# Twelve sigmoids of the second block as one Tanh pass each, and the meta tokens' state products on four row groups

## The reference

```python
proj = jnp.einsum('btd,dk->btk', u, w_in[l])
gates = jax.nn.sigmoid(proj[..., OFF_GATE:])
c = conf_a * jax.nn.sigmoid(conf_g)                 # the GLU
c = depthwise_conv(c, w_conf_dw[l], b_conf_dw[l])   # 31 taps
c = jax.nn.silu(layer_norm(c, conf_ln_g[l], conf_ln_b[l]))
branch_conf = jnp.einsum('btc,cd->btd', c, w_conf_out[l])
xbc = jax.nn.silu(depthwise_conv(xbc, w_ssm_conv[l], b_ssm_conv[l]))   # 7 taps
y = bidir_ssd(xs, dt_raw, ssm_dt_bias[l], ssm_a_log[l], Bs, Cs, ssm_d[l])
y = rms_norm_2(y * jax.nn.silu(z), w_ssm_norm[l])
branch_ssm = jnp.einsum('btc,cd->btd', y, w_ssm_out[l])
merged = gates[..., :D_MODEL] * branch_conf + gates[..., D_MODEL:] * branch_ssm
h = h + jnp.einsum('btd,de->bte', merged, w_out[l])
```

## Time and profile before

| | before |
|---|---|
| median of three runs | 1831.09 us |
| profiled execution, its own time | 1831.83 us |
| its span | 1830.1 us |
| TensorE busy with matmuls | 1724.3 us (94%) |
| VectorE busy | 708.0 us (39%) |
| ScalarE busy | 585.8 us (32%) |
| read from memory | 521.12 MB |

### The profile page before, as it was taken

How to read it: one execution, slowest core, us unless ns; L and a number is a source line. 1 busy time by engine, 2 the same in 40 slices (tenths; PEclk the granted TensorE clock), 3 DMA queues, 4 the chain that set the end, 5 groups by cost and what they waited for, 6 DMA issues and landing times.

```text
span 1830.1 us, 21256 instructions
## 1 busy us (share of the span) xinstructions
PE 1724.3 (94%) x8462; PEld 982.1 (54%) x8462; DVE 708.0 (39%) x1365; ACT 585.8 (32%) x1026; POOL 32.2 (2%) x58
## 2 busy tenths in 40 slices
PE   9999999999999999999999999998989889898997
PEld 8878788887878787777722322222222222222222
DVE  2584466603769999961221111122111211112112
ACT  1153132202365564650133332223222332223222
POOL 4000000000000000000000000000000000000000
PEclk9999999999999999999999999889999999999898
DMA  5340244442443434266879999999999999999996
GB/s 185 116 182 14 80 161 145 170 156 103 166 164 121 158 137 154 104 237 248 322 312 429 431 428 434 429 430 429 431 432 427 433 428 432 432 429 428 431 433 260
DMA packets 34511, 523.47 MB, mean 286 GB/s; under 512 B 3768, under 2 KB 3960, under 8 KB 6392
## 3 DMA queue, kind: packets, MB, share of 16 engines
q1 hardware_dynamic: 33200, 511.75, 68.2%
q10 hardware_dynamic: 1224, 10.50, 1.6%
HBM read 521.12 MB, written 1.12 MB: 285 GB/s over the span
## 4 chain that ended last, share of the span: by engine, by line
PE 60%; DMA 16%; DVE 14%; DVEq 3%; ACT 2%; another core or an unknown queue 2%; issue 1%; ACTq 0%; SPq 0%
PE psum L1181 18%; DMA arena<-in_experts 16%; PE psum L580 10%; PE psum L1153 9%; PE psum L926 5%; DVE arena L2065 4%; PE psum L899 4%; DVE arena L2053 2%; PE psum L1008 2%; PE psum L1165 2%; DVEq L2067 2%; PE psum L664 1%; PE psum L643 1%; PE psum L879 1%
## 5 line engine op out<-in xcount | busy, mean ns | idle before, releaser
L1181 PE MATMUL psum<-arena 128*34 128x512 f32 x2048 | 467.4, 609 | 43.6 <-DMA arena<-in_experts 38.7
L926 PE MATMUL psum<-arena 128*128 128x272 f32 x1344 | 313.9, 393 | 1.6 <-DVE arena L2273 1.6
L1181 PEld LDWEIGHTS psum<-arena 128*34 128x34 f32 x2048 | 120.9, 114 | 362.1 <-issue 313.8
L1692 DVE SCALAR_TENSOR_TENSOR arena<-psum,arena 34x512 f32<-34x512 f32 x64 | 44.2, 690 | 683.4 <-ACT arena L1253 683.4
L926 PEld LDWEIGHTS psum<-arena 128*128 128x128 f32 x1344 | 254.3, 190 | 56.5 <-DVE arena L2273 2.1
L1153 PE MATMUL psum<-arena 128*34 128x512 f32 x1024 | 249.1, 642 | 19.4 <-DMA arena<-in_experts 18.5
L580 PE MATMUL psum<-arena 128*128 128x256 f32 x992 | 215.4, 378 | 0.0
L580 PEld LDWEIGHTS psum<-arena 128*128 128x128 f32 x992 | 187.2, 189 | 27.6 <-issue 1.2
L1153 PEld LDWEIGHTS psum<-arena 128*34 128x34 f32 x1024 | 66.3, 119 | 189.9 <-issue 188.6
L1652 ACT ACTIVATE arena<-psum 34x512 f32<-34x512 f32 x64 | 37.9, 593 | 311.9 <-PE psum L1181 311.9
L2065 DVE SCALAR_TENSOR_TENSOR arena<-arena 128x272 f32<-128x272 f32 x240 | 112.1, 527 | 3.5
(11 more groups left out here) (427 smaller groups left out, 1439.3 us busy)
## 6 DMA issues: line engine op xcount, KB each, us to landing
arena<-in_experts SPq DMA_DIRECT2D x74, 4096.0 KB, 50.4
arena<-in_panels SPq DMA_DIRECT2D x91, 1024.0 KB, 4.8
arena<-in_experts SPq DMA_DIRECT2D x41, 2048.0 KB, 43.8
arena<-in_down_panels SPq DMA_DIRECT2D x8, 1408.0 KB, 6.1
arena<-scr ACTq DMA_DIRECT2D x4, 2176.0 KB, 9.1
arena<-in_experts SPq DMA_DIRECT2D x5, 1024.0 KB, 8.0
arena<-in_experts SPq DMA_DIRECT2D x2, 512.0 KB, 47.8
out<-arena SPq DMA_DIRECT2D x4, 256.0 KB, 2.1
```

The source lines that it names most:

```text
L926: ins = mm(pair[k][:, b, 0:T], slot8[k][:, c, b * P:(b + 1) * P], src[:, c, :], start=c == 0, stop=c == DC - 1)
L1181: ins = mm(psum[lo:lo + CAP, p % 2, :], xg[:, c, :], r_up[2 * p + x][:, c, :], start=c == 0, stop=c == DC - 1)
```

## The change

Two things change, both in the second block. First, every sigmoid but the one behind the layer norm becomes one Tanh of half the argument: sigmoid(x) = (1 + tanh(x/2)) / 2. ScalarE's Abs, Exp, Ln and second Exp become one Tanh (`half_tanh`), VectorE's subtraction goes, and its product becomes a product with the sum in it, (t + 1) * x, as one three-operand instruction. The halves go elsewhere: into the weights of both convolutions and one bias, which VectorE scales once at the start (two instructions of 248 and 192 elements), and into products that were there anyway (`gated`, `ssm_part`, the merge). Tanh is not in the table set that holds Ln, so ScalarE loads the set with Exp and Tanh behind the Ln of dt, and the old one ahead of the Ln of the norm behind the groups.

Second, `ssm_y` does the meta tokens' products ahead of the others, each with its 32 rows only, on row groups 0, 32, 64 and 96 of the array and into four banks.

```diff
...
@@ -430,7 +430,7 @@
                 if g == 1:
-                    sp.wait_ge(ev("gsig_ready"), after["gsig_ready"] + 2)
+                    sp.wait_ge(ev("gates_tanh"), after["gates_tanh"] + 2)
                     expert_panel(0, 10)
@@ -980,14 +980,16 @@
                 for b in range(4):
+                    rows = slice(32 * b, 32 * b + 32)
+                    mm(G[b][:, 0:T], xf[rows, 0, b * P:(b + 1) * P], m_f0[rows, :], start=True, stop=False, skip_group_check=True)
+                for b in range(4):
                     bank = G[b]
...
                             h = 2 * b + x
-                            mm(bank[64 * x:64 * x + 64, lo:hi], src[:, ck, h * 64:(h + 1) * 64], m[:, h, :],
-                               start=at == 0, stop=False, skip_group_check=True)
-                    ins = mm(bank[:, 0:T], xf[:, 0, b * P:(b + 1) * P], m_f0, start=False, stop=True, skip_group_check=True)
+                            ins = mm(bank[64 * x:64 * x + 64, lo:hi], src[:, ck, h * 64:(h + 1) * 64], m[:, h, :],
+                                     start=False, stop=at == 3, skip_group_check=True)
                     ins.then_inc(ev("y_done"), 1)
@@ -1465,9 +1467,9 @@
-            def arg_exp(tmp, name, count, done):
-                act.wait_ge(ev(name + "_arg"), count)
-                A(tmp, tmp, ACT.Exp).then_inc(ev(done), 1)
+            def half_tanh(tmp, x, done, scale=0.5):
+
+                A(tmp, x, ACT.Tanh, scale=scale).then_inc(ev(done), 1)
@@ -1510,8 +1512,8 @@
-            def z_ln(g):
-                sigmoid_ln(zt if g < 3 else zt_last, zT[:, 4 * g:4 * g + 4, :], "z")
+            def z_tanh(g):
+                half_tanh(zt if g < 3 else zt_last, zT[:, 4 * g:4 * g + 4, :], "z_tanh")
@@ -1528,6 +1530,7 @@
             A(dtw, dtw, ACT.Ln).then_inc(ev("dt_ln"), 1)
+            nc.scalar.preload_act_table_set("exp_and_others")
             act.wait_ge(ev("dtr_ready"), 1)
@@ -1543,9 +1546,8 @@
             act.wait_ge(ev("conv6"), after["conv6"] + 1)
-            sigmoid_ln(six, gq[0], "group")
+            half_tanh(six, gq[0], "six_tanh", 1.0)
             copy_mid(MID_OPEN[4:5])
-            arg_exp(six, "group", 1, "sig6")
             for g, bank in enumerate((G[0], G[1], G[3], G[2])):
@@ -1555,14 +1557,12 @@
                     act.drain()
-                    sigmoid_ln(glu_t, glu_gate(g), "glu")
+                    half_tanh(glu_t, glu_gate(g), "glu_tanh")
                 differences(g, 0)
...
                 own_decays(g)
-                if g < 2:
-                    arg_exp(glu_t, "glu", g + 1, "glu_exp")
                 copy_mid(MID_A[g][1:2])
@@ -1573,14 +1573,12 @@
                 act.wait_ge(ev("conv6"), after["conv6"] + g + 2)
-                sigmoid_ln(six, gq[(g + 1) % 2], "group")
+                half_tanh(six, gq[(g + 1) % 2], "six_tanh", 1.0)
                 copy_mid(MID_B[g][0:1])
...
                 act.drain()
-                z_ln(g)
-                arg_exp(six, "group", g + 2, "sig6")
+                z_tanh(g)
                 copy_mid(MID_B[g][1:2])
-                arg_exp(zt, "z", g + 1, "z_exp")
                 if g == 2:
@@ -1594,18 +1592,14 @@
             copy_mid(MID_A[3][1:2])
-            z_ln(3)
+            z_tanh(3)
             copy_mid(MID_A[3][2:3])
-            arg_exp(zt_last, "z", 4, "z_exp")
-            sigmoid_ln(gate_t, gts[:, 0:DC, :], "gates")
+            half_tanh(gts[:, 0:DC, :], gts[:, 0:DC, :], "gates_tanh")
             copy_mid(MID_A[3][3:4])
-            act.wait_ge(ev("gates_arg"), 1)
-            A(gts[:, 0:DC, :], gate_t, ACT.Exp).then_inc(ev("gsig_ready"), 1)
             squares(3)
             act.drain()
-            sigmoid_ln(gate_t, gts[:, DC:2 * DC, :], "gates")
-            act.wait_ge(ev("gates_arg"), 2)
-            A(gts[:, DC:2 * DC, :], gate_t, ACT.Exp).then_inc(ev("gsig_ready"), 1)
+            half_tanh(gts[:, DC:2 * DC, :], gts[:, DC:2 * DC, :], "gates_tanh")
+            nc.scalar.preload_act_table_set("natural_log_exp_and_others")
             act.wait_ge(ev("ssum_done"), after["ssum_done"] + 1)
@@ -1617,8 +1611,7 @@
             act.drain()
-            sigmoid_ln(conf_t, cc, "conf")
-            arg_exp(conf_t, "conf", 1, "csig_ready")
+            sigmoid(conf_t, cc, "conf").then_inc(ev("csig_ready"), 1)
             for i in range(4):
@@ -1718,6 +1711,8 @@
             TT(ident4, ident[:, 0:16], ident[:, 32:48], ADD)
+            for at, count in ((PAR["conf_w"], 248), (PAR["ssm_w"], 192)):
+                TS(par[:, at:at + count], par[:, at:at + count], 0.5, None, MUL)
             dve.drain()
@@ -2071,12 +2066,12 @@
             def glu_mul(x):
-                dve.wait_ge(ev("glu_exp"), after["glu_exp"] + x + 1)
-                TT(cpad[:, 4 * x:4 * x + 4, 15:15 + T], glu(x)[:, :, 0, :], glu_t, MUL).then_inc(ev("cpad_ready"), 1)
+                dve.wait_ge(ev("glu_tanh"), after["glu_tanh"] + x + 1)
+                STT(cpad[:, 4 * x:4 * x + 4, 15:15 + T], glu_t, 1.0, glu(x)[:, :, 0, :], ADD, MUL).then_inc(ev("cpad_ready"), 1)
             def silu(g):
-                dve.wait_ge(ev("sig6"), after["sig6"] + g + 1)
-                TT(gq[g % 2], gq[g % 2], six, MUL).then_inc(ev("g6_ready"), 1)
+                dve.wait_ge(ev("six_tanh"), after["six_tanh"] + g + 1)
+                STT(gq[g % 2], six, 1.0, gq[g % 2], ADD, MUL).then_inc(ev("g6_ready"), 1)
@@ -2172,13 +2167,13 @@
                 zg = zT[:, 4 * g:4 * g + 4, :]
-                dve.wait_ge(ev("z_exp"), after["z_exp"] + g + 1)
-                TT(zg, zg, tmp, MUL)
+                dve.wait_ge(ev("z_tanh"), after["z_tanh"] + g + 1)
+                STT(zg, tmp, 1.0, zg, ADD, MUL)
...
                 dve.drain()
-                TT(zg, zg, gq[g % 2][:, 0:4, :], MUL).then_inc(ev("yz_ready"), 1)
+                STT(zg, zg, 0.5, gq[g % 2][:, 0:4, :], MUL, MUL).then_inc(ev("yz_ready"), 1)
@@ -2187,15 +2182,12 @@
             meta_tables()
-            sigmoid_arg(six, gq[0], "group", 1)
             silu(0)
...
                 ssm_x(g, 2)
-                if g < 2:
-                    sigmoid_arg(glu_t, glu(g)[:, :, 1, :], "glu", g + 1)
                 ssm_e(g)
@@ -2208,10 +2200,8 @@
                 conf_taps(TAPS[g][2])
-                sigmoid_arg(six, gq[(g + 1) % 2], "group", g + 2)
+                silu(g + 1)
                 conf_taps(TAPS[g][3])
-                silu(g + 1)
-                sigmoid_arg(zt, zT[:, 4 * g:4 * g + 4, :], "z", g + 1)
                 conf_taps(TAPS[g][4])
@@ -2226,17 +2216,14 @@
             ssm_m(3)
-            sigmoid_arg(zt_last, zT[:, 12:16, :], "z", 4)
             conf_taps(TAPS[3][2])
             z_silu(3, zt_last)
-            sigmoid_arg(gate_t, gts[:, 0:DC, :], "gates", 1)
             ssm_out(3)
...
             fold(cc)
-            sigmoid_arg(gate_t, gts[:, DC:2 * DC, :], "gates", 2)
             centre()
@@ -2246,11 +2233,11 @@
                 part = gts[:, DC + 2 * i:DC + 2 * i + 2, :]
-                TT(part, part, pair[(base + i) % 2][:, :, 0:T], MUL).then_inc(copied[(base + i) % 2], 2)
-
-            dve.wait_ge(ev("gsig_ready"), after["gsig_ready"] + 2)
+                STT(part, part, 0.5, pair[(base + i) % 2][:, :, 0:T], MUL, MUL).then_inc(copied[(base + i) % 2], 2)
+
+            dve.wait_ge(ev("gates_tanh"), after["gates_tanh"] + 2)
             dve.wait_ge(ev("srs_ready"), after["srs_ready"] + 1)
-            TT(gts[:, DC:2 * DC, :], gts[:, DC:2 * DC, :], ssum.unsqueeze(1).to_broadcast([P, DC, T]), MUL)
+            STT(gts[:, DC:2 * DC, :], gts[:, DC:2 * DC, :], 1.0, ssum.unsqueeze(1).to_broadcast([P, DC, T]), ADD, MUL)
             dve.wait_ge(ev("sq_ready"), SQ["conf"] + 1)
@@ -2268,9 +2255,9 @@
                 part, of_conf = gts[:, DC + 2 * i:DC + 2 * i + 2, :], gts[:, 2 * i:2 * i + 2, :]
-                TT(of_conf, of_conf, pair[k][:, :, 0:T], MUL).then_inc(copied[k], 1)
-                dve.drain()
-                TT(bcf[:, 2 * i:2 * i + 2, :], of_conf, part, ADD).then_inc(ev("merged_ready"), 1)
+                STT(of_conf, of_conf, 1.0, pair[k][:, :, 0:T], ADD, MUL).then_inc(copied[k], 1)
+                dve.drain()
+                STT(bcf[:, 2 * i:2 * i + 2, :], of_conf, 0.5, part, MUL, ADD).then_inc(ev("merged_ready"), 1)
             base += 4
...
             v.memset(pos_t, 0.0)
```

More of the change, by code:

```diff
@@ L106 @@
              "g6_ready": ("g6_ready", 0), "gathered": ("dec_done", 2), "gathered_half": ("bias_ready", 1),
-             "glu_exp": ("rn_ln", 4), "gsig_ready": ("o_copied", 2), "h_ready": ("qk_ready", 1),
+             "glu_tanh": ("rn_ln", 4), "gates_tanh": ("o_copied", 2), "h_ready": ("qk_ready", 1),
              "hacc_turned": ("expG_done", 1), "htok_copied": ("probsT_copied", 6),
@@ L115 @@
              "rows_ready": ("st1_done", 1), "rst_ready": ("gsum_done", 1), "scattered": ("scattered", 0),
-             "sig6": ("ro_ready", 1), "sq_added": ("u_done", 2), "sqx_added": ("eps_ready", 1),
```

(3 more changed lines are left out.)

## The result

Beside each other on one chip, the changed kernel takes 1810.8 us (median of 4 runs, 1808.0 to 1814.9) and the kernel before 1833.65 us (4 runs): a ratio of 0.989, with a 95% interval of 0.9876 to 0.9903. On a second chip it was 1809.29 against 1831.43, ratio 0.9879 (0.9862 to 0.9895). The gain of 20 to 23 us is above the 16 that were forecast, and above the 14 to 19 that had 0.60. The profiled execution took 1808.04 us with a span of 1806.3, which is 23.8 us less than before.

A forecast was written before the change was run, and what follows sets the result against it. TensorE, plus its waits for VectorE, sets the pace of the groups; the weight stream bounds the experts. Waits of 9.5 and meta products of 6.4 make 15.9 us off 1831.83: 1815.9, median said as 1815, range 1808 to 1824.

The forecast's parts named there:

- the 14 to 19 that had 0.60: Main forecast for the whole kernel: gain 14 to 19 us, 1812 to 1817, chance 0.60, larger row-group overlap included.
- The waits: TensorE's five waits for VectorE: four inside the groups go, the variance sum's nearly, plus lower-clock time; 9.5 us.
- The leads: VectorE ahead of TensorE at `m_ready` in the groups: 4.7, 4.2 and 4.9 us, so the waits inside go.
- the waits move: Rival: late copies or decays hold the fourth group again; gain 10.3 or 6 us, 1821 to 1825; chance 0.14.
- The tangent: Sigmoids: Tanh priced like other ScalarE functions, VectorE's product with the sum like the plain one; nothing counted beyond the waits.
- Table loads: ScalarE's two added loads, behind dt's Ln and after the last gate: both hidden in idle time, 0 us.
- The meta tokens' products: In `ssm_y`, four products on row groups: 1.6 us saved per group, 6.4 in all, bounds 0.8 and 2.2.
- The sum: Whole kernel: waits 9.5 plus meta products 6.4 make 15.9 us, from 1831.83 to 1815.9; median said as 1815.
- No overlap: Rival on `ssm_y`: row groups bring no overlap; 12.7 us less, 1818.4, or 1821 with new-shape cost; chance 0.17.
- Nothing arrives: Rival: the experts' weight stream ends the kernel and its start does not move; 1831; chance 0.06.
- A slower clock behind `ssm_y`: Rival: quarter-row products lower TensorE's clock in the panels behind; 1845 at 30 us of such work; chance 0.03.

The follow-up runs named there:

- the tangent alone: The changed kernel with the `ssm_y` of before, so only the sigmoids' part: 1819.81 us against 1830.51, ratio 0.9946.
- the experiment with 24 more: The changed kernel with a table set change and back ahead of each of twelve Tanh, 24 extra loads: 1810.13 us in one run.
- the row groups alone: The kernel before with the new `ssm_y`, sigmoids as before: 1831.21 us against 1830.51, ratio 1.0005.

## Why the prediction was right, and where its sizes were off

**The waits: 9.5 forecast, 10.8 measured** (the tangent alone). The mechanism held to the row: all five gone, the first `ssm_y` at 534.95 (537 forecast). The size was low for two reasons: the idle brackets of the waits inside the groups understate them by 0.1 to 0.3 us each, and the two products behind the longest wait were at the lower clock too, 0.5 us, which I had not counted. Start to start, the pieces of before are longer than those of the changed kernel by 16.76 - 14.82 = 1.94 (bracket 1.87), 2.96 - 1.37 = 1.59 (1.32), 16.67 - 14.83 = 1.84 (1.78), and in the fourth group 4.81 - 1.37 = 3.44 (2.67, and the 0.5); the variance sum 8.63 - 7.55 = 1.08 (1.10). With the 0.89 of the two slow panels that is 10.8. The starts of before that are not in the earlier trace rows are:

```profile
521.97 14.89 PE L926 MATMUL psum<-arena 128*128 128x272 f32 x64
...
600.62 1.08 PE L977 MATMUL psum<-arena 128*128 128x272 f32 x4
...
603.58 14.89 PE L926 MATMUL psum<-arena 128*128 128x272 f32 x64
...
745.50 1.08 PE L977 MATMUL psum<-arena 128*128 128x272 f32 x4
```

**The leads.** VectorE's convolutions start at 530.37, 607.98 and 682.12 (532, 610 and 683 forecast), and the taps in the fourth group's place at 746.89 (747.8 forecast):

```profile
746.89 3.56 DVE L2060 SCALAR_TENSOR_TENSOR arena<-arena 128x272 f32<-128x272 f32 x8
```

The periods between them shrank by 3.9, 2.4 and 2.9 us (81.5, 76.6 and 67.7 before; 77.6, 74.1 and 64.8 now), where the lost subtractions alone were forecast to give 4.2, 3.0 and 3.0. So VectorE's side came close to the forecast. TensorE's did not: `m_ready` leads by 4.6, 2.9 and 4.6 us and in the fourth group by 1.0, where I had 4.7 for the first, 4.2 for the second and 4.9 for the fourth. TensorE asks in the fourth at 747.85 and not at 752.7. It was 2.0 us ahead of my forecast at the first `ssm_y` (1.8 of it the front's clock), and gained 2.9 more up to the fourth, through three `ssm_y` of 0.7 us less each and the waits, which were longer than their brackets. The rival "the waits move" was nearer than its 0.14 says: the product behind the last `x_ready` is done at 730.88 + 0.69 = 731.57, and TensorE asks for it ahead of the third of `ssm_cb`'s products, near 732.6 (731.65 and two products of 0.46). So both margins of the fourth group were 1.0 us, where the sum had given some 5 to the one at `m_ready`.

**The tangent.** One pass of 1632 elements takes 1.56 us like Exp and Ln, and VectorE's product with the sum takes what it did, as the earlier trace rows said.

```profile
546.21 1.56 ACT L1472 ACTIVATE arena<-arena 128x1632 f32<-128x1632 f32 x1 [10.52 <-DVEq L2050]
...
L2074 DVE SCALAR_TENSOR_TENSOR arena<-arena 128x1632 f32<-128x1632 f32 x4 | 7.4, 1858 | 0.2
```

**Table loads: 0 forecast, 0 measured.** The second one is at 761.20, and ScalarE then waits 7.55 us for TensorE's sum; the experiment with 24 more shows how wide the cover is.

```profile
761.20 1.28 ACT L1602 ACT_TABLE_LOAD   x1
770.04 0.49 ACT L1604 ACTIVATE arena<-psum,arena 128x272 f32<-128x272 f32 x1 [7.55 <-PE psum L596]
```

**The meta tokens' products: the term that was mis-sized.** I took 1.6 us per `ssm_y`, 6.4 in all, within bounds of 0.8 and 2.2. They gave 2.31 (8.55 - 6.24), 9.2 in all and outside the bounds. Two things were off. First, I held that the records' order allows only half of an overlap, since a product's second record runs on the same rows as its first. Eight records took 0.67 us, 84 ns each, against 1.93 us with full rows: 2.9 times as fast. The rule of the Trainium skill that I had weighed against it ("TensorE: Matmul & The Clock Gate", section "Measured speedup vs the span model", 3.07 times) was the better guide; the earlier trace rows, with 64-row products of 64 columns, was not the nearest row that I took it for. Second, I counted the cost of alternating at 0.2 us per full product and none in its neighbours, where the 64-column products got 0.4 us shorter too. (The other way, by 0.1: the last of the four full products took 0.57 and not 0.66.)

**The sum.** 10.8 and 4 x 2.31 = 9.2 make 20.0; 19.6 arrived between the two cuts. The 0.4 is in the panels behind each `ssm_y`, which now follow a 64-column product instead of a full one:

```profile
541.19 37.10 PE L926 MATMUL psum<-arena 128*128 128x272 f32 x160
```

These five take 36.93 us (541.19 to 578.12), where the earlier trace rows has 36.83 (547.28 to 584.11), and behind the other three it is 0.1 as well. So one `ssm_y` gave 2.2 us net. The forecast of 15.9 against these 19.6 is what I missed in the terms of my sum; the rest of the profiles' 23.8 us is the clock of the front and the 2.4 behind the groups, of which 2.0 lie in the experts and are open.

**Rivals.** No overlap: refuted by 84 ns per record. Nothing arrives: refuted by the stretch of the experts, 906 us and 22 us earlier. A slower clock behind `ssm_y`: the five panels there take 36.93 us against 36.83, at a granted clock of 1.00.

## What to carry to other kernels

Before a faster TensorE is worth anything, the engine that it waits for has to be ahead: the same 9 us of matmul time were worth 0 alone and 8.8 with VectorE relieved. Products that fill only a part of the rows paid here only when put side by side on different row groups; alone, one of 32 rows cost as much as one of 128. And measure between two rows of the trace that bracket the edit: that distance was the same to 0.01 us in two profiles of the changed kernel, where the whole kernel scatters by several.

## What was not expected of the hardware

- Four fp32 products on 32 rows each, side by side on four row groups, took 0.67 us where one by itself, among other shapes, took 0.65: three came nearly for nothing.
- Matmuls that alternate between two tile shapes cost 1.06 us per `ssm_y`, with eight changes of shape instead of two (an estimate from that: 0.18 us each), and the time is lost in both shapes: 0.66 instead of 0.48 per full product (1.93 for four) and 1.50 instead of 1.39 per eight 64-column ones.
- With the row groups alone, a wait of 3.07 us was followed by 6 us at a granted clock of 0.50, and cost 2.3 us more in the two panels behind it; that of 1.32 us in the same place of the kernel before had no such stretch, its two panels taking 14.89. The wait of 4.89 us in the same kernel cost only 0.9 us in its panels.
- VectorE's products from SBUF ran up to 1.9 times as long beside GpSimd's adds (2.37 against 1.22 us), twelve taps took 7.53 or 6.45 instead of 5.36, and products that read PSUM were not slowed.
